# 8x8 diagonal blocks of the chunk matrices solved on VectorE, in a two-layer hybrid decoder trunk

## The chip, the core and the metric

The kernel runs on one core of one Trainium2 chip. The metric is the device time in microseconds (us). PE is TensorE (matmuls; PEld its weight loads), DVE is VectorE, ACT is ScalarE, POOL is GpSimd, SP is SyncE, which here only issues DMAs.

## What is computed

Two layers over 512 tokens of width 1024, in float32. Each layer mixes four branches; two of them, a gated DeltaNet ("g") and RWKV-7 ("r"), hold a delta-rule state and are computed in chunks of 64 tokens. The part of the reference that matters here, for the g branch:

```
m = jnp.where(strict, jnp.einsum('nbhcd,nbhsd->nbhcs', k_beta, k) * decay, 0.0)
t_inv = lax.linalg.triangular_solve(eye + m, jnp.broadcast_to(eye, m.shape),
                                    left_side=True, lower=True)
u = t_inv @ v_beta
w = t_inv @ (k_beta * jnp.exp(gc)[..., None])
...
qkv = jax.nn.silu(causal_depthwise_conv(qkv, conv_w)).astype(F32)
```

So for every head (4) and chunk (8) the inverse of a 64x64 unit lower triangular matrix is needed, 32 of them for each branch and layer. The r branch is written as a scan in the reference; the kernel brings it to the same chunked form, with the same kind of inverse. The g branch first runs a causal convolution of 4 taps over its 768 channels (six tiles of 128 channels).

## The kernel before, in words

Each engine has its own hand-written program in one block; semaphores tie them together, and every engine takes its work strictly in the order in which the code stands. There is no scheduler.

**The weight stream.** A layer is a list of 134 units (`UNITS`), each 1024x128 of weights. SP loads a unit into `ring` (three slots), ACT rounds it into `w_hi` (`split_next`, L1107), POOL forms `w_lo = ring - w_hi` (L428, two instructions for a unit), and PE multiplies: 16 matmuls of `w_hi` with the high and low parts of the activations (L467, L468), then 8 of `w_lo` (L471). A unit that is a gate of a branch is issued by `gate`; its sum goes through a sigmoid on ACT (`merge_sig`), and `merge_outputs` adds the branch's output projection (L531).

**The chunk matrices.** `transposes` (L584) turns features into token-major tiles in banks `bank_a` (three of them), which ACT copies out in `tok` (L1044, L1047). `pair_matrices` (L597, L598) makes the products of all chunks and heads, two `bank_v` banks a call (four exist, used in turn); DVE masks them out of PSUM in `masked` (L1477). The r branch has four such products (`u`, `akk`, `ark`, `arb`), the g branch two (`u`, `arb`).

**The inverse.** `first_steps` on DVE writes the inverses of the 2x2 diagonal blocks of `u` (the first doubling step is only a mask and an identity: two operations on each half, L1419 and L1484). `invert` then doubles the block size for each `s` in `LEVELS = (2, 4, 8, 16, 32)`: PE computes `y`, DVE masks it (L1493); PE computes the update of the transposed inverse `t`, DVE subtracts it (L1498; left out in the last level); PE computes the update of `x`, DVE subtracts it (L1502). All PE work of it is `chunk_products` (L609), in two halves of eight matrices. Before the first level `t` is made from `x` by PE and copied by ACT (L1032).

**The rest of the branch.** `through` (L645, L646) applies the inverse, then `scan` runs the eight chunks in turn. In it PE fills its gaps with pieces of the next units, DVE has one subtraction (L1516) and one state update (L1522) for each chunk, and ACT copies outputs and runs the sigmoids of the convolution (`conv_sigmoid`).

**The convolution.** `conv(c)` on DVE has four operations on 512 columns for each of the six tiles (L1422, L1425 twice, L1681), and all six stand ahead of the first mask of the r branch. `conv_out(c)` lies in `mg`; `G["zi"]`, written by ACT in chunks 3 and 7 of the r scan, shares tiles 4 and 5 of `mg` with the inputs of convolutions 4 and 5.

**Constants.** One array of 1924 columns is loaded at the start in two DMAs, 256 columns ahead of x, the others behind x and ahead of the first weights, all on SP's queue.

Of the kernel before, what the change touches and what calls it, by code (L numbers as in the profile page):

```python
# [9 lines left out]

# [31 lines left out]
LEVELS = (2, 4, 8, 16, 32)  # L42
INVERSE_STEPS = ("x1", "ti", "y", "t", "x", "wt", "u")
# [44 lines left out]
def _constants():  # L88
# [12 lines left out]
    parts.append(("first_c", half(-1.0 * level(1).T)))  # L101
    for s in LEVELS:
        parts.append((f"level{s}_c", half(level(s))))
    parts += [
        ("eye_c", half(np.eye(P))),
# [55 lines left out]
def build(nc, x_in, pos_in, wstream, par_in, const_in, tabs, x_dram, out):  # L161
    ctx = ExitStack()
    with ctx:
# [91 lines left out]
        for name, n in (  # L255
# [5 lines left out]
            ("r_tok", 8), ("r_mat", 8), ("r_x1", 2), ("r_ti", 2), ("r_y", 10), ("r_t", 8), ("r_x", 10),  # L261
# [5 lines left out]
            ("g_tok", 6), ("g_mat", 4), ("g_x1", 2), ("g_ti", 2), ("g_y", 10), ("g_t", 8), ("g_x", 10),  # L267
# [38 lines left out]
        class Filled:  # L306
# [141 lines left out]
        def _(pe):  # L448
# [12 lines left out]
            def split_product(g, b, hi, lo, sem_name=None, k0=0):  # L461

                s = g % SPLIT
                for k in range(KT):
                    if sem_name:
                        pe.wait_ge(S[sem_name], k0 + k + 1)
                    mm(b[:], w_hi[:, s, k, :], hi[:, k, :], start=k == 0, stop=False)  # L467
                    mm(b[:], w_hi[:, s, k, :], lo[:, k, :], start=False, stop=False)  # L468
                pe.wait_ge(S["split_lo"], g + 1)
# [36 lines left out]
            def gate(l, br, m):  # L506
# [4 lines left out]
                split_product(g, b, h_hi, h_lo).then_inc(a_full, 1)  # L511
                return merges_to(g)
# [239 lines left out]
            for l in range(L):  # L752
# [267 lines left out]
        def _(act):  # L1020
# [149 lines left out]
            for l in range(L):  # L1170
# [231 lines left out]
        def _(dve):  # L1402
# [77 lines left out]
            def first_steps(x, V):  # L1480
                for half in range(2):
                    ms = slice(half * M // 2, (half + 1) * M // 2)
                    tt(V["x"][:, ms, :], V["u"][:, ms, :], wide("first_c"), MUL)
                    v.tensor_tensor(V["x"][:, ms, :], V["x"][:, ms, :], wide("eye_c"), ADD).then_inc(S[x + "_x1"], 1)  # L1484
                    dve.wait_ge(S[x + "_x1"], reached(x + "_x1"))
# [100 lines left out]
            for l in range(L):  # L1586
# [87 lines left out]
                def conv(c):  # L1674
# [3 lines left out]
                    ts(y, G["ci"][:, c, :], pr("conv", 4 * c + 3), None, MUL)  # L1678
                    for j in range(1, 3):
                        stt(y[:, j:T], G["ci"][:, c, 0:T - j], pr("conv", 4 * c + 3 - j), y[:, j:T], MUL, ADD)  # L1680
                    v.scalar_tensor_tensor(y[:, 3:T], G["ci"][:, c, 0:T - 3], pr("conv", 4 * c), y[:, 3:T], MUL, ADD).then_inc(S["g_conv"], 1)  # L1681
                    dve.wait_ge(S["g_conv"], reached("g_conv"))

                for c in range(6):
# [7 lines left out]
                    conv(c)  # L1692
# [15 lines left out]
                scan(l, "r", R, lambda c: None)  # L1708
# [343 lines left out]
```

## Time and profile before

| | before |
|---|---|
| median of 3 runs (lowest to highest) | 2122.13 us (2121.14 to 2122.16) |
| the profiled execution: its time | 2121.77 us |
| its span (first to last instruction) | 2119.9 us |
| PE, DVE, ACT, POOL busy | 97%, 51%, 36%, 35% of the span |
| mean granted TensorE clock | 0.990 of full speed |

The span is 1.87 us less than the time of the same execution. A busy share is an average over both layers; the two layers have the same order of work, and layer 1 reads as layer 0 some 1037.7 us later, so the rows below are those of layer 0.

### The profile page before, as it was taken

How to read it: one execution, taken by the hardware profiler on the slowest of the kernel's cores; microseconds unless marked ns; L12 is line 12 of the kernel's file. 1: busy time of each engine (PE TensorE's matmuls, PEld its weight loads, DVE VectorE, ACT ScalarE, POOL GpSimd, SP SyncE). 2: the span in 40 equal slices, each digit the busy share in tenths (PEclk: the TensorE clock that was granted, in tenths of full speed). 3: DMA queues.
4: the chain of work that ended last, by engine and by line, in shares of the span. 5: the costliest groups of instructions: out<-in, count | busy, mean ns of one | idle time of the engine just before them, and what ended most of it. 6: DMA issues, size and time to landing. Idle time of an engine off the chain costs nothing.

```text
span 2119.9 us, 34678 instructions
## 1 busy us (share of the span) xinstructions
PE 2046.7 (97%) x14608; PEld 1574.7 (74%) x14608; DVE 1084.8 (51%) x1782; ACT 756.4 (36%) x1180; POOL 737.0 (35%) x550
## 2 busy tenths in 40 slices
PE   5999999999999999999989999999999999999997
PEld 4788787756667888888867877876566678888886
DVE  6694654796843422222367844458967343222223
ACT  4541613344353432322253243133443434332322
POOL 2430303331313444444435122133222344444442
PEclk8999999999999999999999999999999999999998
DMA  5320111221322323333332111122113223232331
GB/s 188 102 81 15 48 32 61 92 85 38 114 61 70 115 93 99 91 98 96 93 110 86 47 36 56 33 74 95 50 40 125 65 80 100 90 99 95 95 96 63
DMA packets 52266, 170.04 MB, mean 80 GB/s; under 512 B 5648, under 2 KB 13968, under 8 KB 51600
## 3 DMA queue, kind: packets, MB, share of 16 engines
q1 hardware_dynamic: 50928, 162.75, 24.1%
q0 software_dynamic: 1184, 5.07, 0.6%
q8 instruction: 117, 1.92, 0.4%
q14 instruction: 37, 0.30, 0.0%
HBM read 160.45 MB, written 7.34 MB: 79 GB/s over the span
## 4 chain that ended last, share of the span: by engine, by line
PE 84%; DVE 11%; ACT 3%; issue 1%; DMA 1%; SPq 0%; DVEq 0%; ACTq 0%
PE bank_a L467 13%; PE bank_a L468 12%; PE bank_a L471 12%; PE bank_v L471 7%; PE bank_v L467 7%; PE bank_v L468 7%; PE bank_v L609 5%; PE bank_v L531 4%; DVE mg L1425 1%; DVE arena L1419 1%; PE bank_a L739 1%; PE bank_f L563 1%; PE bank_f L569 1%; PE bank_f L542 1%; PE bank_a L728 1%
## 5 line engine op out<-in xcount | busy, mean ns | idle before, releaser
L428 POOL TENSOR_TENSOR w_lo<-ring,w_hi 128x512 fp32r<-128x512 f32 x536 | 730.6, 1384 | 1263.2 <-ACT w_hi L1107 1263.1
L467 PE MATMUL bank_a<-h_hi,w_hi 128*128 128x512 f32 x1312 | 531.0, 405 | 6.7 <-ACT w_hi L1107 6.7
L468 PE MATMUL bank_a<-h_lo,w_hi 128*128 128x512 f32 x1312 | 512.7, 391 | 0.0
L1107 ACT ACTIVATE w_hi<-ring 128x1024 fp32r<-128x1024 f32 x268 | 281.6, 1051 | 222.4 <-DVE arena L1951 220.1
L471 PE MATMUL bank_a<-h_hi,w_lo 128*128 128x512 f32 x1312 | 324.1, 389 | 0.0
L467 PEld LDWEIGHTS bank_a<-h_hi,w_hi 128*128 128x128 f32 x1312 | 247.2, 188 | 77.7 <-issue 19.4
L468 PEld LDWEIGHTS bank_a<-h_lo,w_hi 128*128 128x128 f32 x1312 | 247.3, 188 | 58.3 <-issue 8.1
L471 PEld LDWEIGHTS bank_a<-h_hi,w_lo 128*128 128x128 f32 x1312 | 246.3, 188 | 51.2
L467 PE MATMUL bank_v<-parts,w_hi 128*128 128x512 f32 x640 | 254.5, 398 | 1.4 <-DVE parts L1922 1.4
L468 PE MATMUL bank_v<-parts,w_hi 128*128 128x512 f32 x640 | 253.4, 396 | 0.0
L1419 DVE TENSOR_TENSOR sg<-bank_v,sg 128x512 f32<-128x512 f32 x112 | 77.5, 692 | 327.3 <-PE bank_v L471 256.3
L1941 DVE TENSOR_TENSOR arena<-arena 128x512 f32<-128x512 f32 x64 | 44.3, 692 | 245.2 <-ACT arena L1383 245.1
L471 PE MATMUL bank_v<-parts,w_lo 128*128 128x512 f32 x640 | 162.2, 395 | 0.0
L467 PEld LDWEIGHTS bank_v<-parts,w_hi 128*128 128x128 f32 x640 | 120.3, 188 | 32.8 <-DVE parts L1922 4.0
L468 PEld LDWEIGHTS bank_v<-parts,w_hi 128*128 128x128 f32 x640 | 120.2, 188 | 29.4 <-issue 0.5
L471 PEld LDWEIGHTS bank_v<-parts,w_lo 128*128 128x128 f32 x640 | 120.2, 188 | 29.1
L1419 DVE TENSOR_TENSOR arena<-arena 128x512 f32<-128x512 f32 (+3 forms) x78 | 101.5, 1302 | 33.9 <-ACT arena L1184 25.7
L609 PE MATMUL bank_v<-arena 64*64 64x64 f32 x3712 | 111.9, 219 | 5.1 <-DVE arena L1493 5.0
L609 PEld LDWEIGHTS bank_v<-arena 64*64 64x64 f32 x3712 | 110.6, 135 | 6.1 <-DVE arena L1493 5.7
L531 PE MATMUL bank_v<-yo,out_ring 128*128 128x512 f32 x256 | 114.7, 594 | 0.0
L1383 ACT ACTIVATE arena<-bank_a 128x512 f32<-128x512 f32 x64 | 38.3, 598 | 205.7 <-PE bank_a L471 205.7
L1077 ACT ACTIVATE sg<-bank_a 128x512 f32<-128x512 f32 x52 | 31.1, 598 | 214.2 <-PE bank_a L471 214.2
(281 smaller groups left out, 2430.2 us busy)
## 6 DMA issues: line engine op xcount, KB each, us to landing
ring<-in_w SPq DMA_DIRECT2D x268, 512.0 KB, 3.5
out_ring<-in_w SPq DMA_DIRECT2D x64, 128.0 KB, 3.5
x_dram<-arena SPq DMA_DIRECT2D x2, 2048.0 KB, 8.9
arena<-x_dram SPq DMA_DIRECT2D x2, 2048.0 KB, 9.8
arena<-in_x SPq DMA_DIRECT2D x2, 1024.0 KB, 8.1
arena<-tabs POOLq DMA_DIRECT2D x4, 512.0 KB, 4.5
out_x<-arena SPq DMA_DIRECT2D x2, 1024.0 KB, 4.3
par<-in_par POOLq DMA_DIRECT2D x2, 937.0 KB, 7.1
```

The lines of the kernel that those rows point to most:

```text
L428: ins = nc.gpsimd.tensor_tensor(w_lo[:, g % SPLIT, ks, :], raw, w_hi[:, g % SPLIT, ks, :].bitcast(F32), ALU.subtract)
L467: mm(b[:], w_hi[:, s, k, :], hi[:, k, :], start=k == 0, stop=False)
L468: mm(b[:], w_hi[:, s, k, :], lo[:, k, :], start=False, stop=False)
L471: ins = mm(b[:], w_lo[:, s, k, :], hi[:, k, :], start=False, stop=k == KT - 1)
L531: ins = mm(b[:], out_ring[:, n % OUT_RING, k, :], yo[:, slot, k, :], start=k == 0, stop=k == 1)
L542: mm(b[:], hi[:, k, :], h_hi[:, k, :], start=k == 0, stop=False)
L609: ins = mm(b[quarter(p_), k * C:(k + 1) * C], lhs[quarter(p_), m, :], rhs(m, p_), start=True, stop=True)
L1077: act_fn(sg[:, n % GATES, :], b[:], ACT.Sigmoid).then_inc(S["mg_sig"], 1)
L1107: act_fn(w_hi[:, g % SPLIT, :, :], ring[:, g % RING, :, :], ACT.Copy).then_inc(S["split_hi"], 1)
L1383: act_fn(relu[:, n % 2, :], b[:], ACT.Relu).then_inc(S["up_relu"], 1)
L1419: link(v.tensor_tensor(out_, a, b, op))
L1941: v.tensor_tensor(relu2[:, n % 2, :], relu[:, n % 2, :], relu[:, n % 2, :], MUL).then_inc(S["up_sq"], 1)
```

## The change

It does five things, in both branches unless one is named.

1. `LEVELS` becomes (8, 16, 32). The 8x8 diagonal blocks are inverted by `block_columns` and `block_inverses` on DVE, by column elimination: the blocks are gathered into a compact form of 16 x 8 columns (a mask and a `tensor_reduce` whose input is read with a step of 8), PE spreads the rows of each block over its partitions with seven matmuls by constant matrices (`spread_rows`), and DVE runs seven multiplications and seven subtractions, each on what the one before wrote, then two operations that write the blocks back into `x`. `first_steps` is gone.
2. `spread_rows` stands inside a gate (`between`), behind its 16 matmuls of `w_hi` and ahead of the 8 of `w_lo`.
3. The pair matrices of `u` stand ahead of all transposes, and the next pair behind the first transposed tile.
4. Convolutions 4 and 5 are cut into eight steps, which DVE takes in the r scan, one or two behind each state update. ACT waits for five convolutions instead of six in chunk 3.
5. The constants grow from 1924 to 2636 columns (712 more), in the second DMA.

```diff
-LEVELS = (2, 4, 8, 16, 32)
+LEVELS = (8, 16, 32)
+BLOCK = 8
...
+    parts.append(("blocks_c", half(i // BLOCK == j // BLOCK)))
+    parts.append(("eye_b", (i % BLOCK == j)[:, :BLOCK]))
+    for k in range(BLOCK - 1):
+        parts.append((f"row{k}", i == j // BLOCK * BLOCK + k))
...
+        def compact(V, i):
+
+            n = M * BLOCK
+            return V["y"].rearrange("p m c -> p (m c)")[:, i * n:(i + 1) * n].rearrange("p (m c) -> p m c", c=BLOCK)
...
+            def spread_rows(l, x, V):
+
+                b, reader, emptied = banks.next("v", x + "_e")
+                pe.wait_ge(reader, emptied)
+                pe.wait_ge(S[x + "_uc"], at(l, x + "_uc", 1))
+                uc, at_ = compact(V, 0), 0
+                for k in range(BLOCK - 1):
+                    n = M * (BLOCK - 1 - k)
+                    ins = mm(b[:, at_:at_ + n], cst(f"row{k}"), uc[:, :, k + 1:BLOCK], start=True, stop=True)
+                    at_ += n
+                ins.then_inc(v_full, 1)
...
-                transposes((R["et"], R["rm"][:, 4:6, :], R["bh"], R["kh"]), "r")
                 pair_matrices(R["bd"], R["et"], "r")
+                transposes((R["et"],), "r")
                 pair_matrices(R["kd"], R["et"], "r")
-                numbers = [gate(l, 2, 0)]
+                transposes((R["rm"][:, 4:6, :], R["bh"], R["kh"]), "r")
+                numbers = [gate(l, 2, 0, lambda: spread_rows(l, "r", R))]
...
-                transposes((G["et"], G["vb"], G["bh"]), "g")
                 pair_matrices(G["co"][:, 2:4, :], G["kb"], "g")
+                transposes((G["et"],), "g")
                 pair_matrices(G["co"][:, 2:4, :], G["co"][:, 0:2, :], "g")
-                numbers.append(gate(l, 2, 7))
+                transposes((G["vb"], G["bh"]), "g")
+                numbers.append(gate(l, 2, 7, lambda: spread_rows(l, "g", G)))
...
-                        act.wait_ge(S["g_conv"], at(l, "g_conv", 6))
+                        act.wait_ge(S["g_conv"], at(l, "g_conv", 5 if c == 3 else 6))
...
+            def block_columns(x, V):
+
+                tt(V["x"], V["u"], cst("blocks_c").unsqueeze(1).to_broadcast([P, M, C]), MUL)
+                v.tensor_reduce(compact(V, 0), V["x"].rearrange("p m (b j) -> p m j b", j=BLOCK), AX_X, ADD).then_inc(S[x + "_uc"], 1)
+
+            def block_inverses(x, V):
+
+                xc = compact(V, 1)
+                link(v.tensor_copy(xc, cst("eye_b").unsqueeze(1).to_broadcast([P, M, BLOCK])))
+                dve.wait_ge(v_full, filled.next())
...
+                for k in range(BLOCK - 1):
+                    n = BLOCK - 1 - k
+                    product = compact(V, 2)[:, :, 0:n]
+                    ins = v.tensor_tensor(product, b[:, at_:at_ + M * n].rearrange("p (m c) -> p m c", c=n),
+                                          xc[:, :, k:k + 1].to_broadcast([P, M, n]), MUL)
...
+                    tt(xc[:, :, k + 1:BLOCK], xc[:, :, k + 1:BLOCK], product, SUB)
...
-                for c in range(6):
+                for c in range(4):
...
+                late_steps = chain(conv(4), conv(5))
+
+                def late_conv(c):
+
+                    for _ in range(2 if c == 0 else 1 if c < 7 else 0):
+                        next(late_steps)
...
                 dve.wait_ge(S["r_tok"], at(l, "r_tok", 8))
+                block_columns("r", R)
                 masked("r", R["akk"], lambda hp: wide("before_c"))
-                first_steps("r", R)
+                block_inverses("r", R)
```

**DVE between the last convolution and the inverse of the r branch.** In the program before (`gsm` is the decay of the g branch, L1477 the masks, the four lines on `consts` behind it are `first_steps`):

```order
82 L1425 SCALAR_TENSOR_TENSOR gsm<-gsm,sml 128x16
83 L1477 TENSOR_TENSOR arena<-bank_v,consts 128x8x64 x4
84 L1419 TENSOR_TENSOR arena<-arena,consts 128x512
85 L1484 TENSOR_TENSOR arena<-arena,consts 128x512
86 L1419 TENSOR_TENSOR arena<-arena,consts 128x512
87 L1484 TENSOR_TENSOR arena<-arena,consts 128x512
88 L1477 TENSOR_TENSOR arena<-bank_v,consts 128x8x64 x4
89 L1493 TENSOR_TENSOR arena<-bank_v,consts 128x512 x2
```

The same place in the changed program, whose line numbers are its own (L1502 is the mask now, L1508 the reduction, L1519 and L1444 a step of the elimination, L1531 the writing back):

```order
74 L1450 SCALAR_TENSOR_TENSOR gsm<-gsm,sml 128x16
75 L1502 TENSOR_TENSOR arena<-bank_v,consts 128x8x64 x2
76 L1444 TENSOR_TENSOR arena<-arena,consts 128x1024
77 L1508 TENSOR_REDUCE arena<-arena 128x128
78 L1502 TENSOR_TENSOR arena<-bank_v,consts 128x8x64 x2
79 L1513 COPY arena<-consts 128x128
80 L1519 TENSOR_TENSOR arena<-bank_v,arena 128x16x7
81 L1444 TENSOR_TENSOR arena<-arena 128x16x7
...
92 L1519 TENSOR_TENSOR arena<-bank_v,arena 128x16
93 L1444 TENSOR_TENSOR arena<-arena 128x16
94 L1531 TENSOR_TENSOR arena<-arena,consts 128x512 x2
95 L1502 TENSOR_TENSOR arena<-bank_v,consts 128x8x64 x4
```

Four operations of 512 columns become 19, of which 14 are a chain of small ones, and the masks of `ark` and `arb` stay behind them.

**PE in the gate that stands ahead of the inverse of the r branch,** in the changed program (L477 and L482 are what L468 and L471 were, L631 is `spread_rows`, L608 and L609 the pair matrices of `ark`):

```order
360 L477 MATMUL bank_a<-h_lo,w_hi 128x512
361 L631 MATMUL bank_v<-arena,consts 128x112
362 L631 MATMUL bank_v<-arena,consts 128x96
363 L631 MATMUL bank_v<-arena,consts 128x80
364 L631 MATMUL bank_v<-arena,consts 128x64
365 L631 MATMUL bank_v<-arena,consts 128x48
366 L631 MATMUL bank_v<-arena,consts 128x32
367 L631 MATMUL bank_v<-arena,consts 128x16
368 L482 MATMUL bank_a<-h_hi,w_lo 128x512 x8
369 L608 MATMUL bank_v<-arena 64x64
```

And before, at the same place:

```order
360 L471 MATMUL bank_a<-h_hi,w_lo 128x512 x8
361 L597 MATMUL bank_v<-arena 64x64
```

The seven matmuls are in the middle of the gate, so the `w_lo` part and all behind it wait for the reduction on DVE.

## Rows read from the trace of the kernel before

**Rows 1.** The page: span, busy time by engine, and the chain by engine.

```profile
span 2119.9 us, 34678 instructions
...
PE 2046.7 (97%) x14608; PEld 1574.7 (74%) x14608; DVE 1084.8 (51%) x1782; ACT 756.4 (36%) x1180; POOL 737.0 (35%) x550
...
PE 84%; DVE 11%; ACT 3%; issue 1%; DMA 1%; SPq 0%; DVEq 0%; ACTq 0%
```

**Rows 2.** Chain that ended last, longest pieces: start us, us, what.

```profile
153.49 23.02 PE bank_v L609 x768
...
244.15 5.36 PE bank_a L848 x48
...
262.77 3.43 PE bank_v L531 x8
```

**Rows 3.** Timeline of DVE, r branch: start, us, what, [idle before <-releaser].

```profile
148.12 1.69 DVE L1484 TENSOR_TENSOR arena<-arena,consts 128x512 f32<-128x512 f32 x1
149.85 2.87 DVE L1477 TENSOR_TENSOR arena<-bank_v,consts 128x512 f32<-128x512 f32 x4
...
154.69 0.69 DVE L1498 TENSOR_TENSOR arena<-arena,bank_v 128x512 f32<-128x512 f32 x1 [0.65 <-PE bank_v L609]
...
166.07 0.69 DVE L1498 TENSOR_TENSOR arena<-arena,bank_v 128x512 f32<-128x512 f32 x1 [0.32 <-PE bank_v L609]
```

**Rows 4.** Timeline of PE, r branch, from the transposes to the inverse.

```profile
132.31 1.51 PE L584 MATMUL bank_a<-consts,arena 128*128 128x128 f32 x12
...
138.57 0.27 PE L597 MATMUL bank_v<-arena 64*64 64x64 f32 x1
...
140.60 0.50 PE L467 MATMUL bank_a<-h_hi,w_hi 128*128 128x512 f32 x1
...
144.36 1.98 PE L471 MATMUL bank_a<-h_hi,w_lo 128*128 128x512 f32 x8
```

**Rows 5.** Timeline of ACT, r branch.

```profile
134.90 2.41 ACT L1044 ACTIVATE arena<-bank_a 64x512 f32<-64x512 f32 x4
137.34 2.06 ACT L1047 ACTIVATE arena<-bank_a 128x512 f32<-128x512 f32 x4
...
146.86 1.05 ACT L1107 ACTIVATE w_hi<-ring 128x1024 fp32r<-128x1024 f32 x1
```

**Rows 6.** Timeline of POOL, both branches.

```profile
147.99 2.95 POOL L428 TENSOR_TENSOR w_lo<-ring,w_hi 128x512 fp32r<-128x512 f32 x2 [10.92 <-ACT w_hi L1107]
...
273.32 2.50 POOL L428 TENSOR_TENSOR w_lo<-ring,w_hi 128x512 fp32r<-128x512 f32 x2 [6.29 <-ACT w_hi L1107]
```

**Rows 7.** Groups of DVE by shape: line, op, shapes, count, busy us, mean ns.

```profile
L1419 DVE TENSOR_TENSOR gsm<-ab,par 128x16 f32<-128x16 f32 x2 | 0.4, 176 | 0.1
L1631 DVE TENSOR_TENSOR arena<-arena 128x1024 f32<-128x1024 f32 x2 | 2.5, 1226 | 0.1
L1825 DVE TENSOR_REDUCE sml<-arena 128x1 f32<-128x512 f32 x2 | 1.4, 687 | 0.1
L1465 DVE RECIPROCAL sg<-sg 128x512 f32<-128x512 f32 x2 | 6.7, 3354 | 0.1
```

**Rows 8.** Timeline of PE and DVE, g branch.

```profile
273.78 1.63 PE L584 MATMUL bank_a<-consts,arena 128*128 128x128 f32 x12 [0.77 <-ACT arena L1047]
...
281.73 0.69 DVE L1484 TENSOR_TENSOR arena<-arena,consts 128x512 f32<-128x512 f32 x1
...
291.57 0.69 DVE L1498 TENSOR_TENSOR arena<-arena,bank_v 128x512 f32<-128x512 f32 x1 [0.42 <-PE bank_v L609]
...
302.99 0.69 DVE L1498 TENSOR_TENSOR arena<-arena,bank_v 128x512 f32<-128x512 f32 x1 [0.32 <-PE bank_v L609]
```

**Rows 9.** Timeline of DVE in the r scan.

```profile
202.52 0.50 DVE L1516 TENSOR_TENSOR un_z<-arena,bank_v 64x128 f32<-64x128 f32 x2 [1.80 <-PE bank_v L667]
```

**Rows 10.** The start: ACT's timeline; a window's busy us by engine, PEclk, DMA share, GB/s.

```profile
15.98 1.06 ACT L1107 ACTIVATE w_hi<-ring 128x1024 fp32r<-128x1024 f32 x1 [2.06 <-DMA ring<-in_w]
...
12.00:16.00 4.00, 1.35 (x13) 1.12 (x11) 3.47 (x8) 1.94 (x8) 0.00 (x0) 1.00 1.02 337
```

More of the change, by code:

```diff
@@ L9 @@
 from contextlib import ExitStack
+from itertools import chain
 import numpy as np
@@ L41 @@
 RW_ORDER = (6, 7, 2, 3, 0, 1, 4, 5)
[L42 to L43 removed]
+LEVELS = (8, 16, 32)
+BLOCK = 8
+INVERSE_STEPS = ("uc", "e", "x1", "ti", "y", "t", "x", "wt", "u")
 GDN0, MLA0, RWK0, DSA0, GATE0 = 0, 1032, 1448, 2472, 3824
@@ L100, in _constants @@
     level = lambda s: (i // (2 * s) == j // (2 * s)) & (i % (2 * s) >= s) & (j % (2 * s) < s)
-    parts.append(("first_c", half(-1.0 * level(1).T)))
+    parts.append(("blocks_c", half(i // BLOCK == j // BLOCK)))
+    parts.append(("eye_b", (i % BLOCK == j)[:, :BLOCK]))
+    for k in range(BLOCK - 1):
+        parts.append((f"row{k}", i == j // BLOCK * BLOCK + k))
     for s in LEVELS:
@@ L104, in _constants @@
     parts += [
-        ("eye_c", half(np.eye(P))),
         ("before_c", half(i < j)),
@@ L459, in begin_unit, with split_product @@
                 return g
-            def split_product(g, b, hi, lo, sem_name=None, k0=0):
+            def split_product(g, b, hi, lo, sem_name=None, k0=0, between=None):
                 s = g % SPLIT
@@ L468, in split_product @@
                     mm(b[:], w_hi[:, s, k, :], lo[:, k, :], start=False, stop=False)
+                if between:
+                    between()
                 pe.wait_ge(S["split_lo"], g + 1)
@@ L504, in token_root, with gate @@
                 ins.then_inc(v_full, 1)
-            def gate(l, br, m):
+            def gate(l, br, m, between=None):
                 g = begin_unit(("merge", br, m), l)
@@ L510, in gate @@
                 pe.wait_ge(reader, emptied)
-                split_product(g, b, h_hi, h_lo).then_inc(a_full, 1)
+                split_product(g, b, h_hi, h_lo, between=between).then_inc(a_full, 1)
                 return merges_to(g)
@@ L1478, in masked @@
                     dve.wait_ge(S[x + "_mat"], reached(x + "_mat"))
-            def first_steps(x, V):
+            def block_columns(x, V):
[5 more added lines that the diff above has]
+                dve.wait_ge(v_full, filled.next())
+                b, at_ = filled.bank(), 0
+                for k in range(BLOCK - 1):
[3 more added lines that the diff above has]
+                                          xc[:, :, k:k + 1].to_broadcast([P, M, n]), MUL)
+                    if k == BLOCK - 2:
+                        ins.then_inc(S[x + "_e"], 1)
+                        dve.wait_ge(S[x + "_e"], reached(x + "_e"))
+                    else:
+                        link(ins)
+                    tt(xc[:, :, k + 1:BLOCK], xc[:, :, k + 1:BLOCK], product, SUB)
+                    at_ += M * n
                 for half in range(2):
                     ms = slice(half * M // 2, (half + 1) * M // 2)
-                    tt(V["x"][:, ms, :], V["u"][:, ms, :], wide("first_c"), MUL)
-                    v.tensor_tensor(V["x"][:, ms, :], V["x"][:, ms, :], wide("eye_c"), ADD).then_inc(S[x + "_x1"], 1)
+                    shape = [P, M // 2, C // BLOCK, BLOCK]
+                    v.tensor_tensor(V["x"][:, ms, :].rearrange("p m (b j) -> p m b j", j=BLOCK), xc[:, ms, :].unsqueeze(2).to_broadcast(shape),
+                                    cst("blocks_c").rearrange("p (b j) -> p b j", j=BLOCK).unsqueeze(1).to_broadcast(shape), MUL).then_inc(S[x + "_x1"], 1)
                     dve.wait_ge(S[x + "_x1"], reached(x + "_x1"))
@@ L1691, in _ @@
                         ts(ab[:, :, 8:16], ab[:, :, 8:16], float((8 * 64) ** -0.5), None, MUL)
-                    conv(c)
+                    for _ in conv(c):
+                        pass
+                late_steps = chain(conv(4), conv(5))
+                def late_conv(c):
+                    for _ in range(2 if c == 0 else 1 if c < 7 else 0):
+                        next(late_steps)
                 dve.wait_ge(S["g_sp"], at(l, "g_sp", 1))
@@ L1706, in _ @@
                     v.tensor_scalar(R["y1"][:, 2 * half:2 * half + 2, :], b[:].rearrange("p (t n) -> p t n", n=256), -1.0, None, MUL).then_inc(S["r_y1"], 1)
-                scan(l, "r", R, lambda c: None)
+                scan(l, "r", R, late_conv)
                 for f in range(2):
@@ L1763, in _ @@
                 masked("g", G["u"], lambda hp: of_parity(G["d"], hp))
+                block_columns("g", G)
                 masked("g", G["arb"], lambda hp: of_parity(G["d"], hp))
-                first_steps("g", G)
+                block_inverses("g", G)
                 merge(l, True)
```

7 lines of the change are left out of this document (5 added, 2 removed).

## The prediction

> **What bounds the kernel now.** I read the page first: PE is busy for 97% of the span, and 84% of the chain that ended last is PE's [rows 1]. So what PE no longer does is gained nearly whole, if nothing else becomes late where it stood. The list of the chain's longest pieces shows the inverses as such PE stretches: 768 instructions of L609 in 23.02 us [rows 2]. Next come the timelines of the engines around one inverse of each branch. In the r branch (layer 0) the operations of DVE on `t` start at 154.69 in the first level and at 166.07 two levels later, each after a short wait for PE: PE sets the pace, at (166.07 - 154.69) / 2 = 5.69 us a level [rows 3]. In the g branch 291.57 and 302.99 give 5.71 [rows 8].
>
> Just ahead of the r inverse it is different. PE waits for DVE and begins the first `t` products at 153.49 [rows 2]. DVE had finished `first_steps` at 148.12 + 1.69 = 149.81, then took four masks (2.87) and the first mask of the inverse. So the start of `t` comes 3.68 us behind the end of the last write of `x`, and that write is on the path [rows 2, 3]. In the g branch `first_steps` ends at 282.42 [rows 8], while PE still has the end of the gate and two output projections (four matmuls as the 3.43 of L531 [rows 2]) ahead of it: there it has slack.
>
> **The levels taken away.** Levels 2 and 4 are two full periods in each inverse, the ones with three products. r: 11.38, g: 11.42. Two layers: 2 x (11.38 + 11.42) = **45.6 us**. DVE, ACT and the banks turn in the same manner in the levels left, so I cost their start the same.
>
> **What DVE must do instead.** No row has the elimination itself. DVE operations of 16 columns take 0.176 us and of 1024 columns 1.226 [rows 7], so 0.159 + 1.042 ns a column. The products and subtractions have 112, 96, ... 16 columns: 448 together, twice. 14 x 0.159 + 896 x 0.00104 = 3.16, and with the 0.03 us that DVE's rows leave between two linked operations 3.6 us. Bounds: all at the price of 16 columns 14 x 0.206 = 2.9; all at 112 columns, 14 x 0.306 = 4.3. I take 3.6. The mask of `block_columns` is 1.23 [rows 7]. The reduction of 1024 columns: a reduction of 512 took 0.687 [rows 7], so 0.69 + 512 x 1.04 ns = 1.22; as far upward as any row goes, the reciprocal of 512 at 3.354 [rows 7] would make 6.7. I take 1.22, since the only reductions in the trace have the slope of every other operation. That row reads its input running on, and this one steps by eight: see the rivals. The copy is 0.2, the writing back 2 x 0.72 as in `first_steps`.
>
> **What PE must do besides.** Seven matmuls of 448 columns together. Float32 matmuls of 128 columns took 5.36 / 24 = 0.22 us each (48 instructions, two a matmul [rows 2]): at most 7 x 0.22 = 1.56. By columns alone, four matmuls of 512 took 3.43 [rows 2], so at least 448 / 512 x 0.86 = 0.75. I take 1.4, near the upper row because each of the 14 passes loads 128 columns of weights of its own.
>
> **r branch, on the clock of layer 0.** The two pairs took 140.60 - 138.57 = 2.03 us together [rows 4]; they now fill places where PE waited for ACT's copies. But these copies are themselves a row of work (134.90 to 139.40 [rows 5]), and the pair put behind the first tile makes the first of them about 1 us late. So I let PE's gate start at 139.6 instead of 140.60, and the last copy, for which `block_columns` waits, end at 140.4 instead of 139.4. DVE is free by then, because two convolutions of four operations (3.3 us) have gone from in front: they end its masks of `u` early, not more. Then: mask and reduction end at 142.9; PE's 16 matmuls of `w_hi` take 144.36 - 140.60 = 3.76 and end at 143.4; spread to 144.8; DVE has meanwhile masked `akk` (1.44) and copied. Elimination from 144.9 to 148.5, writing back to 149.95. That is 0.1 us behind the 149.81 of before.
>
> To it comes POOL. With the first POOL instruction of 147.99 [rows 6] in flight, the operation of DVE at 148.12 took 1.69 instead of 0.69; the masks right behind it, which read PSUM, took 0.72 each as ever [rows 3]. So a DVE operation on SBUF alone waits about 1.0 us for POOL, and one on PSUM doesn't. POOL follows ACT's split, which follows the gate's end. The gate ends at 144.8 + 1.98 = 146.8 against 146.34 before [rows 4], and its split started 0.52 later, POOL 1.13 after that [rows 5, 6]: now about 148.4. The two writes back start at 148.5, both on SBUF, and there are two POOL instructions: +2.0, of which before paid 1.0 (inside the 149.81). The end of `x` comes at 151.95, so **2.1 us** are lost in each r branch, 4.2 in all. If the elimination is a little shorter, one of the two escapes: then 1.1.
>
> The fourth pair now takes the bank of `spread_rows` (the ninth of four in turn) and waits until DVE's last product, about 148.3. What stands behind it is the inverse itself, which waits for `x` anyway: nothing more.
>
> **g branch.** PE's wait of 0.77 between transposes [rows 8] is filled, so gate 7 starts 0.77 earlier; it holds 1.4 more. 0.63 us later than before the inverse can start: 2 x 0.63 = **1.3 us**. DVE, idle before, has the uncovered path: pair at 272.5, masks to 274.0, mask of blocks 1.2 + 1.0 for POOL (273.32 to 275.82 [rows 6]), reduction to 277.5, well before the 280.4 where PE needs it. Spread done at 281.8, elimination to 285.4, `x` complete at 286.9. PE reaches gate 7 at 273.78 + 1.63 + 2.03 - 0.77 = 276.7 and the inverse after 3.76 + 1.4 + 1.9 + 3.43, at 287.1. Nothing is lost, with a cover of 0.2 us for the second half and 0.9 for the first.
>
> **The scan.** Behind each state update DVE idles 1.80 us [rows 9]; a step of the convolution takes 0.5 to 0.75, two in chunk 0 about 1.3, one beside POOL 1.75. All fit: 0. Without that cover 3.3 us a layer would stand in the scan. ACT's chunk 3 asks for convolution 4, done after chunk 2; convolution 5 is done after chunk 6.
>
> **The constants.** 712 columns x 512 bytes = 365 KB more, ahead of the first weights in the queue. ACT waits 2.06 us for the first of them until 15.98, and the DMAs move 337 GB/s in 12 to 16 with all sixteen busy [rows 10]: 365 / 337 = **1.1 us**, once.
>
> **Sum.** 45.6 - 4.2 - 1.3 - 1.1 = 39.0. The profiled execution took 2121.77 (span 2119.9 plus 1.87 around it); 2082.8. The median of the runs is 0.36 above it: 2083.1.
>
> **Rivals.**
> *The reduction is slow.* It reads every eighth word. If each column took twice as long, the reduction would be 1.2 us longer. In the r branch the spread then starts at 144.1 instead of 143.4 and the masks of `akk` and the copy push the elimination 1.2 later; the g branch has 2.9 us of cover. 2 x 1.2 = 2.4: **2085.5**. For it: nothing in the trace reads so; against it: nothing either. By the Trainium skill (Vector Engine (DVE) Microarchitecture Reference, "Measured stream behaviour on trn2") a port runs at full rate only over runs of two or more adjacent words, and a source that hops at every element was measured at 1.73 ns a column, one that steps by 24 words on both sources at 2.5; by that the reduction would take 1.9 to 2.7 us. No row here shows such a read.
> *The lateness in the r branch is not there.* If PE's earlier gate (1.0) comes whole and one write escapes POOL, each r branch loses 0 to 0.5 instead of 2.1: **2079.5**. For it: transposes wait 0.77 at a time, and pairs fill that; against it: the last copy is what `block_columns` waits for.
> *The elimination is long, and the kernel slower.* Place: the 14 linked operations, of which all four inverses wait. It decides at 39.0 us lost: four chains longer by c, the g ones covered for 0.9: 4c - 1.8 = 39, c = 10.2, or 0.73 us more for each operation, 1.0 in all. A wait for POOL costs just that [rows 3], but POOL has two instructions there, not fourteen. At 1.1 us for each operation (15.4 instead of 3.6, c = 11.8): 45.4 lost, **2128.5**. Against it: the 0.176 of the small operations.
> *Nothing gained:* 2122, if the levels left were to end as late as five do now. The steady 5.7 us of each level speak against it (under 1%).
>
> **Chances.** Forecast 45%, slow reduction 30%, no lateness in r 20%, slower by the chain 2%, other small losses (longer steps in the scan, the clock after a wait) 3%. Range 2077 to 2089: the low end is the third case with a spread of 0.75 us (1.3 less in the g branches) and a chain of 2.9 in one layer or so, the high end the slow reduction with the chain at 4.3 in both r branches and 1 us more in each scan. A measurement of this kernel can tell about 0.2% (4.2 us) from no change. Faster by more 97%, within 1%, slower by more 2%.
>
> **What would show it.** L1508, the reduction, at 1.2 us; the 14 operations in 3.6; the write back in POOL's time, 2.7 to 3.4 for two; PE's first wait for DVE ahead of the r inverse up, none new ahead of the g one; the two levels gone at 5.7; ACT's first split 1.1 later; the scans as long as before. The prediction is wrong if a small operation costs much over 0.25, or if PE's granted clock falls while it waits in front of the r inverse.

## The result and the profile after

| | before | changed |
|---|---|---|
| median (lowest to highest) | 2122.05 us (2121.14 to 2122.16) | 2072.98 us (2070.75 to 2073.87) |
| the profiled execution: its time, its span | 2121.77, 2119.9 us | 2073.46, 2071.6 us |
| mean granted TensorE clock | 0.990 | 0.991 |

The ratio is 0.9767, 95% interval 0.9753 to 0.9782: 49.1 us gained where 39.0 were forecast, and 4.0 us below the low end of the range. The page of the changed kernel, to be read against [rows 1]:

```profile
span 2071.6 us, 31700 instructions
...
PE 1995.8 (96%) x13128; PEld 1535.3 (74%) x13128; DVE 1077.2 (52%) x1794; ACT 757.2 (37%) x1180; POOL 737.8 (36%) x550
...
PE 87%; DVE 8%; ACT 3%; issue 1%; DMA 1%; SPq 0%; DVEq 0%; ACTq 0%
```

**Where the time was gained.** ACT loads a table at the same places of both programs, so these rows can serve as milestones. Timeline of ACT, first of the changed kernel, then of the kernel before:

```profile
19.65 1.28 ACT L1144 ACT_TABLE_LOAD   x1
...
214.08 1.28 ACT L1177 ACT_TABLE_LOAD   x1
...
334.35 1.28 ACT L1177 ACT_TABLE_LOAD   x1
...
1040.07 1.28 ACT L1144 ACT_TABLE_LOAD   x1
...
1226.59 1.28 ACT L1177 ACT_TABLE_LOAD   x1
...
1347.02 1.28 ACT L1177 ACT_TABLE_LOAD   x1
...
2051.92 1.28 ACT L1144 ACT_TABLE_LOAD   x1
```

```profile
18.35 1.28 ACT L1119 ACT_TABLE_LOAD   x1
...
220.83 1.28 ACT L1152 ACT_TABLE_LOAD   x1
...
351.87 1.28 ACT L1152 ACT_TABLE_LOAD   x1
...
1063.97 1.28 ACT L1119 ACT_TABLE_LOAD   x1
...
1258.40 1.28 ACT L1152 ACT_TABLE_LOAD   x1
...
1389.08 1.28 ACT L1152 ACT_TABLE_LOAD   x1
...
2100.18 1.28 ACT L1119 ACT_TABLE_LOAD   x1
```

Subtract row from row, changed less before: +1.30 at the start, -6.75 behind the r branch of layer 0, -17.52 behind the g branch, **-23.90 at the end of the layer**, then -31.81, -42.06 and **-48.26**. The g step of layer 0 is -10.77, as forecast (-11.42 + 0.63 = -10.79). The r step is -8.05 where -9.3 was forecast. But between the end of the g branch and the end of each layer, where the change touches no line, another 6.38 and 6.20 us are gained. No term of the prediction stands there.

The groups of PE by shape show what became shorter: the matmuls that read `parts` (the units of `wo` and `down`, whose activations lie in that tile). First of the kernel before, then of the changed one:

```profile
L467 PE MATMUL bank_v<-parts,w_hi 128*128 128x512 f32 x640 | 254.5, 398 | 1.4 <-DVE parts L1922 1.4
L468 PE MATMUL bank_v<-parts,w_hi 128*128 128x512 f32 x640 | 253.4, 396 | 0.0
L471 PE MATMUL bank_v<-parts,w_lo 128*128 128x512 f32 x640 | 162.2, 395 | 0.0
```

```profile
L476 PE MATMUL bank_v<-parts,w_hi 128*128 128x512 f32 x640 | 250.7, 392 | 1.4 <-DVE parts L1983 1.4
L477 PE MATMUL bank_v<-parts,w_hi 128*128 128x512 f32 x640 | 249.0, 389 | 0.0
L482 PE MATMUL bank_v<-parts,w_lo 128*128 128x512 f32 x640 | 158.1, 389 | 0.0
```

On L468 396 ns became 389. Matmuls overlap in these means, so the period says more: the `w_lo` groups of successive units on `parts` start 5.60 us apart before and 5.44 after (a unit is 24 matmuls: 233.3 and 226.7 ns each). The same `w_lo` group on `h_hi` kept 389 ns in both. 80 units x 0.16 = **12.8 us**, where the two stretches gained 12.6.

What sets `parts` apart is its address. `arena` and `parts` begin at the same byte, behind all other tiles, and each tile starts at the next multiple of 32 bytes. Adding up the tiles gives byte 131424 of each partition before (96 past a multiple of 128) and 134272 after (a multiple of 128), since the 712 constant columns take 2848 = 22 x 128 + 32 bytes. `h_hi`, ahead of the constants, starts at 8320, a multiple of 128, in both.

**The r branch, layer 0.** DVE in the changed kernel, for [rows 3]:

```profile
138.73 1.42 DVE L1502 TENSOR_TENSOR arena<-bank_v,consts 128x512 f32<-128x512 f32 x2
142.28 1.23 DVE L1444 TENSOR_TENSOR arena<-arena,consts 128x1024 f32<-128x1024 f32 x1 [2.14 <-ACT arena L1072]
143.54 2.07 DVE L1508 TENSOR_REDUCE arena<-arena 128x128 f32<-128x1024 f32 x1
...
147.58 0.28 DVE L1519 TENSOR_TENSOR arena<-bank_v,arena 128x112 f32<-128x112 f32 x1 [0.38 <-PE bank_v L631]
...
151.02 0.19 DVE L1444 TENSOR_TENSOR arena<-arena 128x16 f32<-128x16 f32 x1
151.24 3.32 DVE L1531 TENSOR_TENSOR arena<-arena,consts 128x512 f32<-128x512 f32 x2
```

The reduction takes 2.07 us, not 1.22; the 14 small operations 151.21 - 147.58 = 3.63 (forecast 3.6); both writes back ran beside POOL (3.32 where 1.42 + 2.0 was forecast). The timelines of POOL, PE and ACT beside it, for [rows 4 to 6]:

```profile
151.07 2.94 POOL L437 TENSOR_TENSOR w_lo<-ring,w_hi 128x512 fp32r<-128x512 f32 x2 [12.62 <-ACT w_hi L1132]
```

```profile
140.15 1.28 PE L595 MATMUL bank_a<-consts,arena 128*128 128x128 f32 x8 [0.56 <-ACT arena L1069]
```

```profile
137.68 2.42 ACT L1069 ACTIVATE arena<-bank_a 64x512 f32<-64x512 f32 x4 [0.97 <-PE bank_a L595]
140.12 2.07 ACT L1072 ACTIVATE arena<-bank_a 128x512 f32<-128x512 f32 x4
```

The last copies start at 140.12 where [rows 5] have 137.34: 2.78 later, 1.3 of it the start. DVE waits 2.14 us for them, and PE still waits for copies. While PE waited ahead of this inverse its granted clock stayed at 1.00 (140 to 160 us of the span).

**The g branch, layer 0.** DVE, with more room ahead of PE:

```profile
267.97 2.20 DVE L1444 TENSOR_TENSOR arena<-arena,consts 128x1024 f32<-128x1024 f32 x1
270.20 2.19 DVE L1508 TENSOR_REDUCE arena<-arena 128x128 f32<-128x1024 f32 x1
...
275.48 0.28 DVE L1519 TENSOR_TENSOR arena<-bank_v,arena 128x112 f32<-128x112 f32 x1 [1.51 <-PE bank_v L631]
...
279.15 1.42 DVE L1531 TENSOR_TENSOR arena<-arena,consts 128x512 f32<-128x512 f32 x2
```

Here DVE waits for PE's spread (L631), which waits for nothing: the reduction's excess is covered.

The mask of the blocks stands beside POOL's instructions of 266.58 and takes 2.20 for the 1.23 of the r branch:

```profile
266.58 2.51 POOL L437 TENSOR_TENSOR w_lo<-ring,w_hi 128x512 fp32r<-128x512 f32 x2 [6.30 <-ACT w_hi L1132]
```

### The profile page after: what moved, and what is told of

It is laid out like the page before. It is cut to its first block, busy times and chain, and to the rows that moved or that the text cites. A ratio compares the mean times of both kernels' runs of the same rounds, so it can differ in the third digit from the quotient of the medians.

```text
span 2071.6 us, 31700 instructions
## 1 busy us (share of the span) xinstructions
PE 1995.8 (96%) x13128; PEld 1535.3 (74%) x13128; DVE 1077.2 (52%) x1794; ACT 757.2 (37%) x1180; POOL 737.8 (36%) x550
## 4 chain that ended last, share of the span: by engine, by line
PE 87%; DVE 8%; ACT 3%; issue 1%; DMA 1%; SPq 0%; DVEq 0%; ACTq 0%
PE bank_a L476 14%; PE bank_a L477 13%; PE bank_a L482 13%; PE bank_v L482 7%; PE bank_v L476 7%; PE bank_v L477 7%; PE bank_v L542 4%; PE bank_v L620 3%; PE bank_a L762 1%; PE bank_f L574 1%; PE bank_f L580 1%; PE bank_f L553 1%; PE bank_a L751 1%; DVE arena L1444 1%; PE bank_f L575 1%
## 5 line engine op out<-in xcount | busy, mean ns | idle before, releaser
L477 PE MATMUL bank_a<-h_lo,w_hi 128*128 128x512 f32 x1312 | 512.7, 391 | 0.0
L482 PE MATMUL bank_a<-h_hi,w_lo 128*128 128x512 f32 x1312 | 324.6, 389 | 0.0
L477 PEld LDWEIGHTS bank_a<-h_lo,w_hi 128*128 128x128 f32 x1312 | 247.3, 188 | 58.2 <-issue 8.1
L482 PEld LDWEIGHTS bank_a<-h_hi,w_lo 128*128 128x128 f32 x1312 | 246.0, 188 | 50.9
L476 PE MATMUL bank_v<-parts,w_hi 128*128 128x512 f32 x640 | 250.7, 392 | 1.4 <-DVE parts L1983 1.4
L477 PE MATMUL bank_v<-parts,w_hi 128*128 128x512 f32 x640 | 249.0, 389 | 0.0
L1444 DVE TENSOR_TENSOR sg<-bank_v,sg 128x512 f32<-128x512 f32 x112 | 77.5, 692 | 317.3 <-PE bank_v L482 245.8
L482 PE MATMUL bank_v<-parts,w_lo 128*128 128x512 f32 x640 | 158.1, 389 | 0.0
L477 PEld LDWEIGHTS bank_v<-parts,w_hi 128*128 128x128 f32 x640 | 120.2, 188 | 25.1 <-issue 0.5
L482 PEld LDWEIGHTS bank_v<-parts,w_lo 128*128 128x128 f32 x640 | 120.1, 188 | 25.0
L1444 DVE TENSOR_TENSOR arena<-arena 128x512 f32<-128x512 f32 (+10 forms) x106 | 107.9, 1018 | 33.5 <-ACT arena L1209 24.3
L542 PE MATMUL bank_v<-yo,out_ring 128*128 128x512 f32 x256 | 114.7, 594 | 0.0
L542 PEld LDWEIGHTS bank_v<-yo,out_ring 128*128 128x128 f32 x256 | 48.0, 189 | 54.5 <-issue 53.0
L620 PE MATMUL bank_v<-arena 64*64 64x64 f32 x2176 | 66.1, 218 | 5.0 <-DVE arena L1541 5.0
```

What stands on the lines that cost most here:

```text
L542: ins = mm(b[:], out_ring[:, n % OUT_RING, k, :], yo[:, slot, k, :], start=k == 0, stop=k == 1)
L1444: link(v.tensor_tensor(out_, a, b, op))
```

## The experiments

Three theories stood against each other for the gain behind the g branch. **Address:** the start of `parts` sets the rate of its matmuls. **Arena:** the address acts through DVE, ACT and POOL on `arena`, and PE is merely waited for less. **Change itself:** the shorter inverse does something to the clock or to the streams later.

### A shift alone, before and after

One unused tile ahead of `arena`, of 8 columns (32 bytes) or 16 (64 bytes):

```diff
+        sb("shift", [P, 8])
         with nc.sbuf_tensor("arena", [P, AQ * T], F32) as arena:
```

The kernel before with 8 columns (`parts` on a multiple of 128):

> The program before, with one unused tile of 32 bytes a partition put ahead of arena and parts, so that both start 32 bytes higher (before they start 32 bytes past a multiple of 64, in the changed program on a multiple of 64). Theory (address): the 1920 fp32r matmuls that read parts drop from 233 to 227 ns apart, 5.60 to 5.44 us for a unit of 24, 80 units: 12.8 us faster, 2109.3. Rival (the step comes from the other edits, as less traffic of DVE or of DMAs beside them): no change, 2122.

Measured: 2108.76 us, ratio 0.9942 (0.9927 to 0.9957), beside 2120.83 of before: -12.1 us, with not one line of the computation changed. The group of `parts` with its low half, for L468 above:

```profile
L469 PE MATMUL bank_v<-parts,w_hi 128*128 128x512 f32 x640 | 249.0, 389 | 0.0
```

That is the row of L477 in the changed kernel to the last digit, in a kernel that has nothing of the change: the third theory falls. The milestones move by -6.09 - 0.34 = -6.43 from the end of the g branch to the end of layer 0, and by -6.43 there in layer 1 too; within the branches of layer 0 they move by 0.1 and 0.4. (Another 1.5 us of this execution lies at the start of layer 1, where the other executions differ from each other by up to 0.9.)

The changed kernel with 8 columns (32 past a multiple of 128):

> The changed program with the same unused 32 bytes: arena and parts start 32 bytes past a multiple of 64 again. Theory (address modulo 64): units on parts back at 5.60 us, 12.8 us slower than the change, 2085.8, which is what the prediction's row on the slow reduction gave (2085.5). Rival (other edits): 2073.

Measured: 2086.38 us, 0.9837 (0.9822 to 0.9852); the units at 5.60 us. The gain is given back: +13.4 by the medians, and 6.44 + 6.47 = 12.9 in the two stretches behind the g branches.

The changed kernel with 16 columns (64 past a multiple of 128):

> The changed program with 64 unused bytes. Theory (modulo 64): as the change, 2073, 5.44 us a unit. Rival (modulo 128 is what counts; parts then starts 64 past a multiple of 128): 5.60 us a unit, 2085.8.

Measured: 2078.19 us, 0.9798 (0.9783 to 0.9812), +5.2 (4.6 in the two stretches), the units at 5.49 to 5.50 us. That is neither the 2073 of the theory nor the 2085.8 of its rival:

```profile
L478 PE MATMUL bank_v<-parts,w_hi 128*128 128x512 f32 x640 | 250.5, 391 | 0.0
```

So a start at 0 is fastest, 64 costs some 2 ns a matmul, and 32 and 96 (before) 6.7 ns.

### Only `parts` moved, `arena` where it was

The tile starts 8 columns earlier than the part of it that is used; four scratch tiles that lie in its shadow move along:

```diff
-        parts = sb("parts", [P, 4, KT, T], F32R)
+        parts = sb("parts", [P, 8 + 4 * KT * T], F32R)[:, 8:].rearrange("p (a k t) -> p a k t", a=4, k=KT)
```

> The changed program with parts alone moved by 32 bytes (and four scratch tiles that share its columns moved with it), arena where it was. Theory (the moving operand of the matmul alone): 5.60 us a unit, 2085.8, all other stages as in the change. Rival (the place of arena, which DVE, ACT and POOL use, is what helps): 2073.

Measured: 2085.32 us, 0.9831 (0.9815 to 0.9847); +12.3 (12.7 in the two stretches).

```profile
L477 PE MATMUL bank_v<-parts,w_hi 128*128 128x512 f32 x640 | 253.4, 396 | 0.0
```

`arena` stood on its multiple of 128 here, and the loss is whole. The arena theory falls.

### The same on the other operand tile

The kernel before with `h_hi` and `h_lo` 32 bytes further, and by the second idle tile all tiles behind them, `w_hi` and `w_lo` too, 64 bytes further:

```diff
+        sb("shift", [P, 8])
         h_hi = sb("h_hi", [P, KT, T], F32R)
...
+        sb("shift2", [P, 8])
```

> The program before with 32 unused bytes ahead of h_hi and 32 behind h_lo: only h_hi and h_lo change their place modulo 64; the tiles behind move by 64. Theory (an fp32r moving operand of 512 columns that starts off a multiple of 64 bytes costs 6.7 ns more): 188 units of 24 such matmuls, 30.1 us slower, 2151. Rival (only parts, which ends in the region of arena, is sensitive): 2121.

Measured: 2145.32 us, 1.0110 (1.0095 to 1.0125): +23.1. Groups by shape, to be read against the 405 and 389 ns of `h_hi` in the kernel before:

```profile
L469 PE MATMUL bank_a<-h_hi,w_hi 128*128 128x512 f32 x1312 | 538.0, 410 | 5.9 <-ACT w_hi L1109 5.9
L473 PE MATMUL bank_a<-h_hi,w_lo 128*128 128x512 f32 x1312 | 332.7, 396 | 0.0
...
L565 PE MATMUL bank_f<-h_hi,w_hi 128*128 128x512 f32 x96 | 41.9, 436 | 4.3 <-ACT sg L1090 4.3
```

These 1312 / 8 = 164 units cost 164 x 0.16 = 26.2, and 24.2 show at the last milestone. The rest of the forecast (30.1) was for 24 other units, of which 20 are taken in the scans; the row of those (`bank_f`) keeps the 436 ns that it has before. Why they don't slow down was not tried. This run also holds two controls. The weights `w_hi` and `w_lo` moved from a multiple of 128 to 64 past one, and the matmuls on `parts` kept their 398, 396 and 395 ns, so 64 bytes at the start of the weights cost nothing there. `parts` itself went from 96 to 32 past, from one slow start to another, so the 23.1 us don't come from it.

**A tile that moved and did not matter.** `yo`, the operand of the output projections (L531 before, L542 after), lies behind the constants as well: it starts on a multiple of 128 before and 32 past one in the changed kernel. Its matmuls are plain float32, not fp32r. Its group in the changed kernel, with the same 114.7 us and 594 ns as L531 has before:

```profile
L542 PE MATMUL bank_v<-yo,out_ring 128*128 128x512 f32 x256 | 114.7, 594 | 0.0
```

So the effect is shown for fp32r operands, and this float32 operand did not have it.

### The levels alone

The kernel before with doubling steps 2 and 4 left out of `invert`, so that it leaves out part of each inverse:

```diff
-LEVELS = (2, 4, 8, 16, 32)
+LEVELS = (8, 16, 32)
```

> The program before with the doubling steps of 2 and 4 left out of all four inverses (the 8x8 blocks keep only their first step, so this leaves out part of the computation), all tiles at their old places. Theory: two full levels of 5.7 us in each inverse are the whole gain and nothing comes late in their place: 45.6 us less than before, 2075.2. Rival (the levels left start later, as ACT's copy of t or the banks are not ready): less than 43 us.

Measured: 2077.37 us, 0.9789 (0.9774 to 0.9803): **-44.9**. The milestones of ACT behind the r and the g branch of layer 0:

```profile
210.59 1.28 ACT L1152 ACT_TABLE_LOAD   x1
...
330.26 1.28 ACT L1152 ACT_TABLE_LOAD   x1
```

-10.24 and -21.61; with the 0.76 by which this execution started later, 11.0 for r and 11.4 for g. In layer 1 the same milestones give 11.63 and 11.39, so the four branches gain 45.4.

### The constants alone

The kernel before with 720 idle columns more. Their 2880 bytes move `parts` from 96 to 32 past a multiple of 128, from one slow start to another:

```diff
-              ("eps", np.full((P, 1), EPS)), ("gn_eps", np.full((P, 1), GN_EPS))]
+              ("eps", np.full((P, 1), EPS)), ("gn_eps", np.full((P, 1), GN_EPS)), ("idle", np.ones((P, 720)))]
```

> The kernel before with 720 idle columns of constants, which move every tile behind them by 2880 bytes, 32 past a multiple of 64 as before. Theory (the start costs by bytes alone): ACT's first split 1.1 to 1.3 us later, nothing else, 2122.1 + 1.2 = 2123.3, with the units on parts at 5.60 us. Rival, that any move of parts by some 2.8 KB makes its matmuls faster, whatever the alignment: 2122.1 + 1.2 - 12.8 = 2110.5.

Measured: 2122.91 us, 1.0005 (0.9996 to 1.0015), beside 2121.47: +1.4 by the medians, which is not clear of the noise. About as many bytes as in the change, and without the alignment nothing of the 12.8: the units stay at 5.60 us. ACT's first split starts at 16.85, 0.9 later than in the kernel before, but `b_shift32`, with no constant more, has it at 16.86. So one execution can't price the transfer. The four kernels with 1924 columns have the first split at 15.98 to 16.86, mean 16.4, and the seven with 2636 columns ahead of the weights at 16.87 to 17.78, mean 17.5: about 1.0.

The changed kernel with the big DMA of constants behind the first two units:

```diff
-            sp.dma_start(consts[:, 2 * P:], const_in[:, 2 * P:]).then_inc(more_here, 16)
...
+                if g == 1:
...
+                    sp.dma_start(consts[:, 2 * P:], const_in[:, 2 * P:]).then_inc(more_here, 16)
```

> The changed kernel with the large DMA of constants (2380 columns) behind the first two weight units in SP's queue instead of ahead of them. Theory: ACT's first split waited 2.64 us for the ring, because the constants stood in front; without them that wait goes and the whole kernel moves forward by it: 2073.0 - 2.6 = 2070.4, with the first split near 14.7 instead of 17.3. Rival, the constants are themselves what is needed next: some engine then waits for them, and at most the 1.3 us that the 712 columns cost come back: 2071.7 or more.

Measured: 2070.45 us, 0.9754 (0.9737 to 0.9770). ACT's timeline at the start:

```profile
14.33 1.99 ACT L1133 ACTIVATE w_hi<-ring 128x1024 fp32r<-128x1024 f32 x2
...
19.43 0.20 ACT L1145 ACTIVATE sml<-sml 128x4 f32<-128x4 f32 x1 [1.81 <-DVE sml L1470]
```

The split is 2.96 earlier than the 17.29 of the changed kernel, but the next step of ACT now waits 1.81 us for DVE, and the milestones of layer 0 behind it are only 1.4 to 1.5 earlier (the last one of the kernel 1.9). About half of the wait came back under another name. The starts of executions scatter by 0.9 us, so the size is rough.

### The reduction as three additions

```diff
-                v.tensor_reduce(compact(V, 0), V["x"].rearrange("p m (b j) -> p m j b", j=BLOCK), AX_X, ADD).then_inc(S[x + "_uc"], 1)
+                tt(V["x"][:, :, 0:32], V["x"][:, :, 0:32], V["x"][:, :, 32:64], ADD)
+                tt(V["x"][:, :, 0:16], V["x"][:, :, 0:16], V["x"][:, :, 16:32], ADD)
+                v.tensor_tensor(compact(V, 0), V["x"][:, :, 0:8], V["x"][:, :, 8:16], ADD).then_inc(S[x + "_uc"], 1)
```

> The changed program with the reduction over eight blocks done by three additions of adjacent halves (512, 256 and 128 columns, read in runs of 8 or more words) instead of tensor_reduce with a step of 8. Theory (the step costs 0.85 us over 1.22): the additions take 0.69 + 0.42 + 0.29 and the gaps, 1.5 us instead of 2.07; PE's wait of 0.54 us ahead of spread_rows in each r branch goes, 1.1 us faster than the change in all, 2072, nothing in the g branch. Rival (the reduction isn't on the path): 2073.0 and the wait stays.

Measured: 2071.19 us, 0.9762 (0.9748 to 0.9777). DVE in the r branch:

```profile
141.46 1.22 DVE L1444 TENSOR_TENSOR arena<-arena,consts 128x1024 f32<-128x1024 f32 x1 [2.14 <-ACT arena L1072]
142.72 1.15 DVE L1444 TENSOR_TENSOR arena<-arena 128x512 f32<-128x512 f32 x2
143.90 0.29 DVE L1510 TENSOR_TENSOR arena<-arena 128x128 f32<-128x128 f32 x1
144.11 1.41 DVE L1502 TENSOR_TENSOR arena<-bank_v,consts 128x512 f32<-128x512 f32 x2
```

From the mask to the next masks 2.65 us instead of 145.53 - 142.28 = 3.25. The milestone behind the r branch of layer 0 comes 0.60 earlier relative to one ahead of it, and 0.90 in layer 1: the reduction was on the path there, as rival 1 has it. In the g branch of layer 0 nothing is gained. The intervals of this kernel and the changed one overlap, so the times alone don't show it. Whether the step of eight or the 128 separate sums make `tensor_reduce` slow was not separated: the only other reductions here write one column, read their input running on, and take 420 and 687 ns for 256 and 512 columns, 1.04 ns a column.

### The order of pairs and transposes

The changed kernel with all transposes ahead of the pairs, in both branches:

```diff
+                transposes((R["et"], R["rm"][:, 4:6, :], R["bh"], R["kh"]), "r")
                 pair_matrices(R["bd"], R["et"], "r")
-                transposes((R["et"],), "r")
                 pair_matrices(R["kd"], R["et"], "r")
-                transposes((R["rm"][:, 4:6, :], R["bh"], R["kh"]), "r")
...
```

> The changed kernel with all transposes ahead of both pairs again, as before. Theory: in the r branch the gate of PE starts 0.6 us later and the last copy, for which the block masks wait, comes 1.4 us earlier; the wait of 0.54 us ahead of the spread goes, so the two cancel (0.1 us later); in the g branch PE's wait of 0.77 us between transposes is back: 2 x (0.1 + 0.8) = 1.8, 2074.8. Rival, the late copies are the whole price of the new order in the r branch: 2 x (0.8 - 1.3) = -1.0, 2072.0.

Measured: 2077.02 us, 0.9791 (0.9776 to 0.9805): +4.0. PE in its g branch:

```profile
267.52 1.63 PE L595 MATMUL bank_a<-consts,arena 128*128 128x128 f32 x12 [0.78 <-ACT arena L1070]
...
275.68 1.71 PE L631 MATMUL bank_v<-arena,consts 128*128 128x112 f32 x14 [0.65 <-DVE arena L1506]
```

The old wait of 0.78 is back, and a second of 0.65 is new: with the pair later, mask and reduction end behind the 16 matmuls of the gate. The g branches are 1.53 and 1.01 longer, the r branches 0.26 and 0.29. The copies, 1.3 earlier here (the table load behind them at 140.87 instead of 142.20), bring nothing, since DVE then waits 2.54 us for the pair instead.

### The convolutions

The changed kernel with all six convolutions ahead of the r masks:

```diff
...
-                for c in range(4):
+                for c in range(6):
...
-                scan(l, "r", R, late_conv)
+                scan(l, "r", R, lambda c: None)
```

> The changed program with convolutions 4 and 5 back in front of the first mask. Theory: DVE then reaches the masks of u about 5.7 us later than in the change, and block_columns starts at about 145.9 instead of 142.3 of layer 0, 3.6 us on the path in each layer: 7.2 us slower than the change, 2080. Rival (the prediction's reading, that these convolutions only end the masks early): no difference, 2073.

Measured: 2082.47 us, 0.9813 (0.9797 to 0.9829): +9.5. DVE:

```profile
145.28 1.42 DVE L1502 TENSOR_TENSOR arena<-bank_v,consts 128x512 f32<-128x512 f32 x2
...
148.00 1.98 DVE L1508 TENSOR_REDUCE arena<-arena 128x128 f32<-128x1024 f32 x1
...
153.35 0.28 DVE L1519 TENSOR_TENSOR arena<-bank_v,arena 128x112 f32<-128x112 f32 x1 [1.79 <-PE bank_v L631]
```

The masks start 6.55 later, but the chain only 5.77. The r branch of layer 0 is 5.2 longer (6.12 - 0.89), that of the second layer about 3.9. Part of that is clock. PE's timeline, then a window's PE busy us, granted clock, DMA share and GB/s:

```profile
150.13 3.12 PE L631 MATMUL bank_v<-arena,consts 128*128 128x112 f32 x14 [4.05 <-DVE arena L1508]
```

```profile
150.00:156.00 6.00, 5.87 (x21) 0.51 0.00 1
```

PE had waited 4.05 us for the reduction, and then the granted clock is 0.51 of full speed, which is the lower of its two levels (1.2 of 2.4 GHz). The spread takes 3.12 us for the 1.71 of the changed kernel, and the eight matmuls of `w_lo` behind it 3.76 for 2.09. In the changed kernel PE waits 0.54 us there and keeps 1.00. So moving two convolutions, which the prediction costed at nothing, keeps DVE early enough, and with it the clock. How much of the 5.2 is the wait and how much the clock was not separated; the two longer pieces come to 3.1 us at most.

### Both improvements

Three additions and the late constants together:

> The changed kernel with the reduction as three additions and the large DMA of constants behind the first two weight units, parts at a multiple of 128 bytes. Theory: the two gains add, 1.8 for the additions and 2.6 for the start: 2073.0 - 4.4 = 2068.6. Rival, no gain at the start: 2071.2.

Measured: 2070.64 us, 0.9758 (0.9744 to 0.9773). Neither of the two, nor both, is shown to be faster than the changed kernel by these intervals.

## Why the prediction was wrong

**The step that failed is "The constants".** It took the 712 columns for a transfer only: 365 KB, 1.1 us. They also lie in memory ahead of `arena` and `parts`, and moved them from 96 past a multiple of 128 to a multiple of 128. That is worth 12 to 13 us, from three sides: the shift alone gains 12.1, taking it from the changed kernel loses 13.4 and 12.3, and the units on `parts` give 12.8. The prediction's sum has no term for it. No row showed it in advance as such; what was there to be seen is that the same 512-column matmuls had two means, 389 to 391 ns on `h_hi` and `h_lo` (L471, L468) and 395 to 396 on `parts`.

Without it the changed kernel takes 2085.3 (`parts` alone moved) or 2086.4, where 2083.1 was forecast. That is inside the range and next to the rival of the slow reduction, 2085.5, which names the main part of the excess in the r branch.

**The terms of the sum,** as measured:

- Levels taken away: 45.6 forecast; 44.9 measured alone, 45.4 by the milestones of that run. Right.
- r branch: 2.1 forecast, 11.0 - 8.05 = 2.95 in layer 0 and about 3.7 in layer 1 (11.63 of the levels alone less 7.91 here). Mis-sized: the reduction, 2.07 for 1.22. The first rival had the place, with 1.2 us for the 0.85 measured: three additions in its stead give back 0.60 and 0.90. Why layer 1 loses 0.7 more than layer 0 stays open. The Trainium skill (Vector Engine (DVE) Microarchitecture Reference, "Measured stream behaviour on trn2") has 1.73 ns a column for one source that hops 4 KiB at every element. The estimate of 1.9 to 2.7 us that the prediction worked out from that section holds the measured 2.07 (2.0 ns a column), which agrees with a cost of the step but, as said above, doesn't separate it. The copies were forecast 1.0 later and were about 1.5; the gate of PE starts 141.35 - 1.3 = 140.05, 0.55 earlier instead of 1.0, since PE still waits for copies between the transposes. The two convolutions moved from in front of DVE's masks take 5.7 us (6.55 - 0.89), not the 3.3 of the prediction; no sum used it.
- POOL in the two writes back: forecast 2.0, measured 3.32 - 1.42 = 1.90. Right.
- The chain: 3.6 forecast, 3.63 measured. The long chain is out: its operations take 0.19 to 0.28.
- g branch: 0.63 forecast, 0.65 measured in layer 0 (11.42 - 10.77), by the levels alone 0.60; about 1.1 in layer 1. The spread takes 1.63 us here and 1.71 in the r branch instead of 1.4; the gate starts 0.64 earlier (7.04 behind the last `w_lo` part of the gate ahead, against 7.68) where 0.77 was forecast.
- The scan: 0 forecast, its chunk period still 3.33 us; right. The step beside POOL took 1.45.
- The constants as a transfer: 1.1 forecast, 1.3 here, about 1.0 by the means of the first splits. Right, as far as the scatter of the start lets one say.

The sum of the measured terms, 44.9 + 12.8 - 6.65 - 1.7 - 1.3 = 48.05, is near the 48.26 of the last milestone. (With the 45.4 of the milestones it would be 48.55: half a microsecond is what such a sum can be trusted to.) The prediction's other sign of being wrong, a granted clock that falls while PE waits ahead of the r inverse, did not appear; it did where the convolutions stood in front.

**What stays open.** Why the start of the streamed fp32r operand matters, and why it doesn't in the units of the scans nor for the float32 `yo`. The start of the weights was moved by 64 bytes only, without effect; 32 was not tried.

## What to carry to other kernels

When a change makes any tile larger, work out where the tiles behind it start before and after: an edit in one place can move a matmul operand elsewhere onto or off a multiple of 128 bytes, for better or worse. If the same matmul shape has two means in one profile, look at the start of what it reads, and put the fp32r operands that are streamed most on a multiple of 128. Where a wait is removed, ask which wait is second: taking 2.96 us from ACT's first split gave about 1.5. And where one grows, look at PE's granted clock behind it.

## What the runs showed of the hardware

- A matmul of 512 fp32r columns follows the one before after 226.7 ns when the tile it streams starts at a multiple of 128 bytes, about 229 at 64 past one, and 233.3 at 32 or 96 past one. In the units of the scans `h_hi` at 32 past a multiple cost nothing (436 ns in both), and the float32 matmuls on `yo` took 594 ns at 0 and at 32.
- A `tensor_reduce` of 1024 columns that steps by eight words takes 1.98 to 2.19 us; the same sum by three additions 1.15 + 0.29 (2.11 + 0.29 where the first ran beside POOL).
- The operation on SBUF of 1024 columns took 2.20 instead of 1.23 us beside POOL's `w_lo` in the g branch, as the writes back did in the r branch; the masks out of PSUM that ran beside POOL kept their 0.7 each.
- After PE had waited 4.05 us the granted clock was 0.51 for the next 6 us (`a_conv_front`); after the waits of up to 0.65 us ahead of the r inverse of the changed kernel it stayed at 1.00.
